# Cached keys turned two pairs at a time, and loaded in four transfers of 128 partitions with 2 KB runs

## What is computed

```python
# attention of 4 heads, each with two halves of 64 dimensions; the sample group:
pk = cache_k[l][page_table].reshape(dec_batch, past_len, H_DIFF, 2 * QK_HEAD_DIM)
pv = cache_v[l][page_table].reshape(dec_batch, past_len, H_DIFF, V_HEAD_DIM)
k_all = jnp.concatenate([pk, k], axis=1); v_all = jnp.concatenate([pv, v], axis=1)

s = jnp.einsum('bqhmd,bkhmd->bhmqk', q, k2) * (QK_HEAD_DIM ** -0.5)
s = jnp.where(dist >= 0, s + bias, NEG_INF)
p = jax.nn.softmax(s, axis=-1)
a = p[:, :, 0] - lam * p[:, :, 1]
out = jnp.einsum('bhqk,bkhd->bqhd', a, v)
```

## Time and profile before

| what | value |
|---|---|
| median of 3 runs | 1327.76 us (1327.72 to 1328.27) |
| the profiled execution's own time | 1327.3 us |
| its span in the trace | 1325.6 us |
| PE busy | 1311.1 us (99%), 8364 matmuls |
| DVE busy | 726.3 us (55%) |
| ACT busy | 446.8 us (34%) |
| DMA | 132424 packets, 146.96 MB, mean 111 GB/s |
| granted TensorE clock | 0.999 |
| chain that ended last | PE 94%, ACT 1%, DVE 1% |

### The profile page before, as it was taken

One profiled execution on the slowest core, in us unless ns is written; L12 is line 12 of the kernel. 1 busy time (PEld: TensorE's weight loads), 2 busy tenths in 40 slices (PEclk: granted clock), 3 DMA queues, 4 the chain that ended last, 5 costly groups with the idle time before them and its releaser, 6 DMA issues.

```text
span 1325.6 us, 21890 instructions
## 1 busy us (share of the span) xinstructions
PE 1311.1 (99%) x8364; PEld 1190.0 (90%) x8364; DVE 726.3 (55%) x1185; ACT 446.8 (34%) x764; POOL 158.2 (12%) x323
## 2 busy tenths in 40 slices
PE   8999999999999999999999999999999999999998
PEld 7999999977667888998989898999989898989986
DVE  6446745268886655556453545455354636453556
ACT  6321001057777443441322232232303131323332
POOL 2027000022222211200000000000000000000003
PEclk9999999999999999999999999999999999999999
DMA  7676778369996241420111102010202011020117
GB/s 246 213 262 232 261 230 214 74 176 261 263 271 218 93 142 50 120 80 17 63 32 56 39 16 79 16 63 16 79 16 74 21 63 32 27 68 16 48 49 139
DMA packets 132424, 146.96 MB, mean 111 GB/s; under 512 B 25852, under 2 KB 101285, under 8 KB 132357
## 3 DMA queue, kind: packets, MB, share of 16 engines
q1 hardware_dynamic: 107865, 122.30, 31.4%
q10 hardware_dynamic: 23500, 20.24, 4.7%
q0 software_dynamic: 992, 3.54, 1.6%
HBM read 114.06 MB, written 31.47 MB: 110 GB/s over the span
## 4 chain that ended last, share of the span: by engine, by line
PE 94%; ACT 1%; DVE 1%; issue 1%; POOL 1%; DMA 0%; SPq 0%; POOLq 0%; DVEq 0%; ACTq 0%
PE PS L2521 40%; PE PS L2239 18%; PE PS L2586 17%; PE PS L2465 7%; PE PS L2289 2%; PE PS L2601 2%; PE PS L2616 2%; PE PS L2329 1%; PE PS L2316 1%; PE PS L2392 1%; PE PS L2362 1%; PE PS L2224 1%; PE PS L2456 1%; PE PS L2372 1%; ACT prob L1102 1%
## 5 line engine op out<-in xcount | busy, mean ns | idle before, releaser
L2521 PE MATMUL PS<-act_lo,wu_hi 128*128 128x364 f32 (+1 forms) x1056 | 346.4, 328 | 0.0
L2521 PE MATMUL PS<-act_hi,wu_lo 128*128 128x364 f32 (+1 forms) x1056 | 346.0, 328 | 0.0
L2521 PE MATMUL PS<-act_hi,wu_hi 128*128 128x364 f32 (+1 forms) x1056 | 345.9, 328 | 0.0
L2521 PEld LDWEIGHTS PS<-act_hi,wu_hi 128*128 128x128 f32 x1056 | 198.5, 188 | 0.5
L2521 PEld LDWEIGHTS PS<-act_lo,wu_hi 128*128 128x128 f32 x1056 | 198.1, 188 | 0.4
L2521 PEld LDWEIGHTS PS<-act_hi,wu_lo 128*128 128x128 f32 x1056 | 198.3, 188 | 0.0
L2004 DVE TENSOR_TENSOR y_acc<-y_acc,PS 128x512 f32<-128x512 f32 x162 | 111.1, 686 | 116.0 <-PE PS L2586 116.0
L2586 PE MATMUL PS<-wd_hi,g_hi 128*128 128x512 f32 x324 | 130.0, 401 | 0.0
L2586 PE MATMUL PS<-wd_lo,g_hi 128*128 128x512 f32 x324 | 128.0, 395 | 0.0
L2586 PE MATMUL PS<-wd_hi,g_lo 128*128 128x512 f32 x288 | 114.0, 396 | 0.0
L1364 ACT CAST g_hi<-conv 128x1088 fp32r<-128x1088 f32 x21 | 23.2, 1102 | 245.6 <-PE PS L2586 189.6
(11 more groups left out here) (294 smaller groups left out, 2293.6 us busy)
## 6 DMA issues: line engine op xcount, KB each, us to landing
wu_raw<-in_w_up_dram SPq DMA_DIRECT2D x44, 512.0 KB, 3.9
k_tok<-in_cache_k_dram SPq DMA_DIRECT2D x64, 256.0 KB, 4.0
keys_t<-k_turned ACTq DMA_DIRECT2D x32, 512.0 KB, 4.3
vpage<-in_cache_v_dram SPq DMA_DIRECT2D x64, 256.0 KB, 5.5
wd_raw<-in_w_down_dram SPq DMA_DIRECT2D x22, 512.0 KB, 5.3
w_raw<-in_w_in_dram SPq DMA_DIRECT2D x20, 512.0 KB, 6.5
kt_mid<-keys_t SPq DMA_DIRECT2D x20, 256.0 KB, 8.7
kt_b<-keys_t SPq DMA_DIRECT2D x20, 256.0 KB, 9.1
```

The costliest lines, as they stand in the source:

```text
L2521: mm = nc.tensor.matmul(PS[:, 3 * half + c, 0:kept(c)], a[:, half, k, :], b[:, k, KEPT[c]], start=(j == 0), stop=(j == len(parts) - 1))
```

## The change

Units of keys take the place of pairs. Both pairs of a unit are turned at the place of the second one (`UNIT_AT`), by four transposes of half the size: first two quarters of the dimensions of both pairs into buffer 0, then the other two into buffer 1. ACT issues the two stores of a unit one behind the other. `keys_t` has the layout unit, i, dimension, j, pair, column, so that for each i a row of one dimension holds 2 KB of a unit in one piece. Each of the four loads of a unit now brings one i for all 128 partitions. The key buffers have i ahead of the pair, and the matmul's view of them follows. A slot of `k_tok` comes free later (the wait in `load_pair`), and two waits of DVE on its own earlier work are added.

```diff
@@ -191,7 +191,7 @@
     k_turned = [at("k_turned0", 2 * ACT_BYTES + 1024, [P, 2 * 512]), at("k_turned1", SCRATCH, [P, 2 * 512])]
-    keys_t = nc.dram_tensor("keys_t", [4 * NB, 4, 32, 4, 2 * H * 32], F32)
+    keys_t = nc.dram_tensor("keys_t", [2 * NB, 4, 32, 4, 2, 2 * H * 32], F32)
@@ -241,7 +241,7 @@
     lo_place = Region(ACT_BYTES, 2 * ACT_BYTES)
-    kt_a, kt_b, kt_mid = (lo_place.put(n, [P, 2, 4, 2, H, 32]) for n in ("kt_a", "kt_b", "kt_mid"))
+    kt_a, kt_b, kt_mid = (lo_place.put(n, [P, 4, 2, 2, H, 32]) for n in ("kt_a", "kt_b", "kt_mid"))
     prob0 = lo_place.put("prob0", [P, 2, SEQ])
@@ -254,7 +254,7 @@
     att = Region(R2, BIAS)
-    kt_first = att.put("kt_first", [P, 2, 4, 2, H, 32])
+    kt_first = att.put("kt_first", [P, 4, 2, 2, H, 32])
     prob1 = att.put("prob1", [P, SEQ])
@@ -267,7 +267,7 @@
     s_prob1 = att.put("s_prob1", [P, 512])
-    kt = [kt_first, at("kt_second", V1, [P, 2, 4, 2, H, 32])] + [kt_mid, kt_b, kt_a] * 5
+    kt = [kt_first, at("kt_second", V1, [P, 4, 2, 2, H, 32])] + [kt_mid, kt_b, kt_a] * 5
     vpage = [vpage0, vpage1]
@@ -665,6 +665,8 @@
+    UNIT_AT = PAIR_AT[1::2]
+
     NORM_AT = [first_of[2] + 1 + s for s in range(STEPS + 1)]
@@ -847,7 +849,7 @@
             if n >= 3:
-                sp.wait_ge(ktok_turned, n - 2)
+                sp.wait_ge(ktok_turned, 4 * ((n - 3) // 2) + 3 + (n - 3) % 2)
             for a in range(2):
@@ -876,10 +878,9 @@
                 sp.wait_ge(sscore_ready, 2 * (u - 3) + 2)
-            for j in range(4):
-                src = bass.AP(keys_t, (2 * u * 4 * 32 * 4 + j) * 256, [[4 * 256, 32], [32 * 4 * 256, 8], [1, 256]])
-                dst = kt[u][32 * j:32 * j + 32].rearrange("a n i p h t -> a (n i) (p h t)")
-                sp.dma_start(dst, src).then_inc(kt_loaded[kt_place(u)], 16)
+            for i in range(4):
+                src = keys_t[u, i].rearrange("d j n c -> j d (n c)")
+                sp.dma_start(kt[u][:, i].rearrange("a n p h t -> a (n p h t)"), src).then_inc(kt_loaded[kt_place(u)], 16)
@@ -1026,11 +1027,12 @@
-        def store_pair(n):
-
-            act.wait_ge(ktok_turned, n + 1)
-            dst = keys_t[n].rearrange("i d j c -> (i d) (j c)")
-            act.dma_start(dst, k_turned[n % 2][:]).then_inc(ktok_stored[n % 2], 16)
+        def store_unit(u):
+
+            for a in range(2):
+                act.wait_ge(ktok_turned, 4 * u + 2 * a + 2)
+                dst = keys_t[u, :, :, 2 * a:2 * a + 2].rearrange("i d j n c -> (i d) (j n c)")
+                act.dma_start(dst, k_turned[a][:]).then_inc(ktok_stored[a], 16)
@@ -1080,8 +1082,8 @@
                 take_job(n)
-            if n - 1 in PAIR_AT:
-                store_pair(PAIR_AT.index(n - 1))
+            if n - 1 in UNIT_AT:
+                store_unit(UNIT_AT.index(n - 1))
@@ -1636,15 +1638,18 @@
-        def turn_pair(n):
-
-            b = TOK_OF[n]
-            dve.wait_ge(slot_loaded[b % 3], slot_count(n))
-            if n >= 2:
-                dve.wait_ge(ktok_stored[n % 2], 16 * (n // 2))
-            blocks = k_tok[b][:].rearrange("p a (h j c) -> p j (a h) c", h=H, c=32)
-            turned = k_turned[n % 2][:].rearrange("p (j n t) -> p j n t", j=4, t=32)
-            nc.vector.transpose(turned, blocks).then_inc(ktok_turned, 1)
+        def turn_unit(u):
+
+            for a in range(2):
+                if u >= 1:
+                    dve.wait_ge(ktok_stored[a], 16 * u)
+                for n in (2 * u, 2 * u + 1):
+                    b = TOK_OF[n]
+                    if a == 0:
+                        dve.wait_ge(slot_loaded[b % 3], slot_count(n))
+                    blocks = k_tok[b][:].rearrange("p a (h j c) -> p j (a h) c", h=H, c=32)[:, 2 * a:2 * a + 2]
+                    turned = k_turned[a][:].rearrange("p (j n x t) -> p j n x t", j=2, n=2, t=32)[:, :, n % 2]
+                    nc.vector.transpose(turned, blocks).then_inc(ktok_turned, 1)
@@ -1690,6 +1695,8 @@
+            if c == 0:
+                dve.wait_ge(dve_took, max(took[n][1] for n, job in enumerate(jobs) if job[0] == "k"))
             if c >= 2:
@@ -1816,8 +1823,8 @@
                 first_steps()
-            if n in PAIR_AT:
-                turn_pair(PAIR_AT.index(n))
+            if n in UNIT_AT:
+                turn_unit(UNIT_AT.index(n))
             if n in ROWS_AT:
@@ -1829,6 +1836,8 @@
             dve.wait_ge(job_ready, n + 1)
+            if n == ROWS_AT[0]:
+                dve.wait_ge(ktok_turned, 4 * (NQ_PAIR // 2) + 4)
             if kind in ("q", "k"):
@@ -2359,7 +2368,7 @@
                 out = PS[32 * h:32 * h + 32, SMP_BANK, ks].rearrange("r (p i t) -> r i p t", p=2, t=32)
-                mm = nc.tensor.matmul(out, qp[:, 2 * pr + b2, h, :], kt[u][:, j % 2, :, :, h, :],
+                mm = nc.tensor.matmul(out, qp[:, 2 * pr + b2, h, :], kt[u][:, :, j % 2, :, h, :],
                                       start=(j % 4 == 0), stop=(j % 4 == 3))
```

## The result

| what | before | after |
|---|---|---|
| median | 1328.01 us (1327.72 to 1328.58, 4 runs) | 1404.38 us (1403.80 to 1405.07, 4 runs) |
| ratio | | 1.0575 [1.0556, 1.0593] |
| profiled execution, its span | 1327.3, 1325.6 | 1404.35, 1402.6 |
| granted clock over the span | 0.999 | 0.973 |

The kernel is 5.75% slower. The forecast was 1405 us.

The account below looks back on a forecast made before the run. PE was taken to bound the kernel, with key transfers hidden. Key waits of 73 us plus 4 for the clock, 77 on the profiled 1327.3, give 1404.3; the median lies 0.5 above: 1405 us, range 1375 to 1475.

Parts of the forecast that it names:

- What bounds the kernel: Whole kernel: PE is busy 99% of the span; key and value transfers in attention are hidden, though DMA is full.
- DVE: Projection: 64 half-size transposes at 0.7 us, 5 us more in all, hidden; most of the 22.6 us store wait goes.
- SP in the projection: Slots come free up to one place (4 to 8 us) later, delaying weights; cover about 16 us, cost 0.
- ACT: Stores of turned keys: same number and size, the last two about 2 us later, cost 0.
- The products: Attention: 256 matmuls read keys at another stride; taken as no cost, upper bound 17 us.
- The key loads: Attention: outermost count 4 puts all keys on four of 16 DMA engines; PE waits 73 us in all.
- by the bytes: Attention: bytes per engine at 23.8 GB/s sum to 196.8 us, so unit 15 is taken 71.0 us late.
- the walk: Attention: following both transfer streams with SP's buffer waits gives PE waits from unit 3 on, 73 us in all.
- The clock: Attention: PE's clock falls in most of the new waits; 4 us taken, bounds 0 and 21.
- All 16 engines: Rival, key loads: packets, not the outermost count, set an engine's share; not slower, 1327.8 us; chance 0.11.
- Four engines at a worse rate or a lasting low clock: Rival, attention: 20 GB/s an engine gives 1436 us, the clock alone 1421, 1432 put for both; chance 0.22.
- Eight engines: Rival, key loads: dealing coarser or finer, for instance eight engines; 1328 to 1340 us, with dearer matmuls 1345; chance 0.05.

Follow-up runs that it names:

- count-128 kernel: Changed kernel with `keys_t` laid out unit, i, j, dimension, so each key load is one 256 KB piece with outermost count 128: 1327.87 us, timed again 1327.68 us.
- the padding: Changed kernel with 217 unused identity matmuls on PE ahead of the late key units: 1402.09 us; an earlier run with 388 took 1412.87 us.
- four transfers of 32: Changed kernel with a unit's four key loads again 32 partitions each, outermost count 32, packets still 2 KB: 1329.41 us.
- on two engines: Changed kernel with each key load cut into two of 64 partitions, whose DRAM view begins with a count of 2: 1544.84 us.
- pieces of 32: Layout of the kernel with outermost count 128, but key loads cut by j into 32 partitions each: 1328.68 us.

## Why the prediction was right, and where its sizes were off

**What bounds the kernel.** Right: PE waited for no transfer before. The count-128 kernel is the proof: its stage has a share of 0.78, and the median stands.

**DVE.** Right in both. The new transposes of 128x512:

```profile
L1652 DVE STREAM_TRANSPOSE k_turned<-k_tok x64: 661/671/715, 52.1 to 225.9; 128x512 f32<-128x512 f32 x64
```

671 ns against the 0.7 us taken, and PE keeps 50.00 of 50 in the projection. The wait for the stores fell from 22.6 us to 12.7; that it would mostly go was too much.

**SP in the projection, ACT.** Right, nothing on the path: unit 2 is taken at 291.65, before at 291.61.

**The products.** 1.07 us for 16 where the clock is full, as before. The bound of +17 was idle.

**The key loads.** The mechanism is right, shown from both sides and at four counts. The first long wait, at unit 3, is 3.69 us (predicted 3.6); then come 9.80 at unit 5 (8.7), 7.84 at 6 (10.6), 9.98 at 9 (9.5) and 10.85 at 13 (9.5). The later ones of each series are shorter than predicted, 4.09 at 10 (7.8), 5.32 at 14 (9.4) and 4.57 at 15 (6.6), which fits that PE comes to them later, out of work at the low clock. Unit 15 is 74.3 us late (71 by the bytes, 73 by the walk). Two terms inside are off:
- A full engine carries 102 / 4 = 25.5 GB/s, not 23.8. A unit takes 10.3 us in place of 11.0, 14 of them 144 in place of 154. The upper bound of the rate, 25.3, was nearly the true one. A 2 KB packet takes 84 ns in the median there.
- Values move at 261 GB/s, not at 381. From 278.4 to 478.5, less 144 for keys and 1.3 for the first packet, 55 us are left for values, weights and any gap in the queue, where the prediction had 41.3. At 261 GB/s the values of six sequences alone take some 48 us by this estimate, where it had 33.0. It took the rate of a store for loads of values; why these are slower no run isolates.

10 too much and 14 too little: that the sum was better than its parts is luck. The share in 300 to 450 came out as 0.52, not "about 0.4", at 170 GB/s where 160 was expected.

**The clock.** This term was mis-sized as the prediction's own accounts had it. It had 73 us of waits and 4 of clock. The trace has 59.0 of waits and 16.3 + 2.3 of slower work. The sum holds because the queue sets the end: what PE does slowly comes out of its waits. What the padding took back of it is 2.3 us in the median and 2.7 in the span, against 4.

**Wrong in what the profile would show.** `vpage` was to land above 5.5 us and landed in 4.9; the reason is open. For the landing of `kt_mid`, which was to be above 15 us, the page has no number. Packets fell by 8960, not 8192.

**The rivals.** All 16 engines: excluded, the share is 0.26. Four engines at a worse rate or a lasting low clock: the rate is excluded, 25.5 GB/s an engine, and the low clock, 0.84 over the stage, cost 2 to 3 us by the run with padding and not the 21 behind the rival's 1421. Eight engines: excluded by the same share.

## What to carry to other kernels

Before a transfer is made "wider", read both access patterns from the outside in: in these runs the outermost count decided how many of the 16 engines carried it, and 128 partitions behind a count of 4 were slower (1404 us) than four transfers of 32 (1329). The sign in a profile is a DMA share that stands at a small fraction (0.52, 0.26, 0.13) while the issuing engine is held for the length of the transfer. Where the rows can lie in one piece, so that the partitions themselves are the outer axis, the wide transfer is worth having (4.1 us to landing against 8.7 before), but its gain reaches the time only if somebody waits for it.

## What the runs showed of the hardware

**The issuing engine is held by a slow queue.** Where the queue was full, at units 3 and 4, a key transfer of 256 KB held SP for 2.5 to 2.6 us on four engines, and unit 3's eight of 128 KB on two engines held it for 20.5 us, 2.6 us each; in the earlier trace rows it was 0.5 to 1.1.

**The same 256 KB, in 2 KB packets over 16 engines, lands in 4.1 us in 128 partitions and in 8.1 in 32**, at 360 and 234 GB/s where only keys move (count 128 and pieces of 32, above).

**The clock's fall and return.** The changed kernel around the wait of unit 5; PE ends at 321.75 and resumes at 331.55:

```profile
321.00:322.00 1.00, 0.75 (x7) 0.54 (x6) 1.00 (x4) 0.47 (x1) 0.00 (x0) 1.00 0.26 100
323.00:324.00 1.00, 0.00 (x0) 0.00 (x0) 0.70 (x3) 0.10 (x2) 0.00 (x0) 0.63 0.78 254
332.00:333.00 1.00, 1.00 (x16) 0.38 (x8) 0.00 (x0) 0.00 (x0) 0.00 (x0) 0.50 0.87 338
336.00:337.00 1.00, 1.00 (x7) 1.00 (x6) 0.60 (x4) 0.79 (x5) 0.00 (x0) 0.55 0.26 107
338.00:339.00 1.00, 1.00 (x48) 1.00 (x40) 0.96 (x4) 0.94 (x6) 0.27 (x2) 1.00 0.26 100
```

The clock is at 2.4 GHz until PE stops, falls to 1.2 GHz in 323 to 324, and comes back only in 336 to 337, about 5 us after PE has resumed; the 16 products of 1.07 us take 1.94 meanwhile. After the waits of 9.80, 9.98 and 10.85 us the clock came back 5.4, 5.6 and 8.3 us after PE resumed. Half of that, 2.7 to 4.1 us, is my estimate of what such a wait costs PE beyond itself. It is paid wherever no queue covers it. The shorter wait at unit 3 cost too: PE idles 3.69 us, resumes at 302.50, and the clock falls at 302.8 and is back at 306.2.
